# A two-layer decoder trunk on eight cores: weight casts issued in other places, the row work of the routing stage queued among the attention steps, and a last stage without a barrier before it

## What is computed

```python
for i in range(2):
    h = rms_norm(x, mix_norm_g[i])
    if i == 0:
        x = x + gmlp_mixer(h, ...)          # 1024 -> 6144 gelu, layer norm, 128x128 spatial mix, 3072 -> 1024
    else:
        k_band, v_band = shared_kv(x, kv_norm_g, w_kv, b_kv)     # previous and own block of 128
        x = x + swa_sink_attention(h, w_q, b_q, sinks, w_o, b_o, k_band, v_band)   # 16 heads of 64
    hn = rms_norm(x, ffn_norm_g[i])
    if i == 0:
        x = x + (silu(hn @ w_gate) * (hn @ w_up)) @ w_down       # 2816 wide
    else:
        x = x + moe_swiglu(hn, ...)          # top 2 of 8 experts, each 3584 wide
    x = x + (p[i] @ ple_w_proj[i]) * sigmoid(rms_norm(x, ple_norm_g[i]) @ ple_w_gate[i])
return rms_norm(x, final_norm_g)
```

## Time and profile before

| | us |
|---|---|
| median of three runs | 4339.06 |
| the runs | 4335.07, 4339.06, 4602.17 |
| the profiled execution, device time | 4306.77 |
| its span on the slowest core, 6 | 4305.2 |
| spans of the eight cores | 4209.3 to 4305.2 |

### The profile page before, as it was taken

One profiled execution on the slowest core, in us unless ns is written; L12 is line 12 of the kernel. 1 busy time (PEld: TensorE's weight loads), 2 busy tenths in 40 slices (PEclk: granted clock), 3 DMA queues, 4 the chain that ended last, 5 costly groups with the idle time before them and its releaser, 6 DMA issues.

```text
span 4305.2 us, 68531 instructions; the slowest of 8 cores (4209.3 to 4305.2 us)
## 1 busy us (share of the span) xinstructions
PE 3491.6 (81%) x20783; PEld 1990.8 (46%) x21030; DVE 1257.3 (29%) x2477; ACT 1030.7 (24%) x2319; POOL 588.5 (14%) x588
## 2 busy tenths in 40 slices
PE   4888848798899546755757999999999999999445
PEld 2555533354456323433653545546464646464222
DVE  2544531122222336745531111111111111111153
ACT  2555520011211322332421111111111111111133
POOL 1111122200000222221011000000010101010132
PEclk8999979899999777877858999999999999999767
DMA  9578769656655995999629897969696969795631
GB/s 158 89 117 129 108 134 229 179 84 97 100 86 91 195 177 80 112 109 109 106 110 259 201 241 172 255 163 265 170 264 173 254 185 255 196 239 141 203 124 59
DMA packets 368662, 691.02 MB, mean 161 GB/s; under 512 B 21642, under 2 KB 289708, under 8 KB 353836
## 3 DMA queue, kind: packets, MB, share of 16 engines
q0 software_dynamic: 280384, 299.40, 49.7%
q1 hardware_dynamic: 69772, 345.26, 24.0%
q10 hardware_dynamic: 18144, 41.95, 2.7%
HBM read 866.00 MB, written 212.21 MB: 250 GB/s over the span
## 4 chain that ended last, share of the span: by engine, by line
PE 71%; DMA 10%; issue 8%; DVE 5%; ACT 3%; POOL 2%; another core or an unknown queue 1%; DVEq 0%; SPq 0%; ACTq 0%; POOLq 0%
PE ps L247 68%; PE ps L250 3%; DMA arena<-xs 3%; DVE arena L270 2%; ACT arena L258 2%; DMA arena<-wgu 2%; DVE arena L261 1%; DMA arena<-gmlp_w_in 1%; ACT L258 1%; DMA xs<-arena 1%; DMA arena<-gmlp_w_out 1%; DMA arena<-ygs,arena 1%; POOL xgs L1354 1%; DMA arena<-gmlp_w_s 1%; POOL arena L291 1%
## 5 line engine op out<-in xcount | busy, mean ns | idle before, releaser
L247 PE MATMUL ps<-arena 128*128 128x512 bf16 (+7 forms) x18889 | 3321.9, 337 | 254.7 <-ACT arena L258 68.3
L247 PEld LDWEIGHTS ps<-arena 128*128 128x128 bf16 (+2 forms) x19136 | 1834.6, 103 | 1703.1 <-issue 454.8
L258 ACT ACTIVATE arena<-ps 128x512 f32<-128x512 f32 (+3 forms) x720 | 369.9, 516 | 1524.0 <-PE ps L247 1501.6
L261 DVE TENSOR_TENSOR arena<-arena,ps 128x512 bf16<-128x512 f32 (+3 forms) x619 | 351.3, 569 | 1239.3 <-PE ps L247 1140.1
L250 PE MATMUL ps<-arena 128*128 128x128 bf16 (+2 forms) x1894 | 210.7, 261 | 540.6 <-DVE arena L270 128.1
L250 PEld LDWEIGHTS ps<-arena 128*128 128x128 bf16 (+2 forms) x1894 | 165.2, 123 | 592.4 <-issue 583.1
L261 POOL TENSOR_TENSOR arena<-arena 128x512 f32<-128x512 f32 (+4 forms) x196 | 263.4, 1356 | 770.2 <-DVE arena L270 356.5
L258 ACT ACTIVATE arena<-arena 128x512 bf16<-128x512 bf16 (+9 forms) x300 | 193.6, 648 | 550.6 <-DMA arena<-xs 360.3
L1439 POOL DMA_DIRECT2D arena<-wdn x120 | 110.5, 925 | 1497.2 <-PE ps L247 1492.6
L275 ACT COPY arena<-ps 128x512 f32<-128x512 f32 (+1 forms) x166 | 134.1, 808 | 752.5 <-PE ps L247 588.3
L277 DVE COPY arena<-ps 128x512 f32<-128x512 f32 (+4 forms) x179 | 101.3, 569 | 696.6 <-PE ps L247 588.8
(11 more groups left out here) (38 smaller groups left out, 280.6 us busy)
## 6 DMA issues: line engine op xcount, KB each, us to landing
arena<-wgu SPq DMA_DIRECT2D x105, 2048.0 KB, 11.7
arena<-wdn POOLq DMA_DIRECT2D x120, 896.0 KB, 26.6
wgu<-moe_w_gate POOLq DMA_DIRECT2D x56, 1024.0 KB, 20.1
wgu<-moe_w_up POOLq DMA_DIRECT2D x56, 1024.0 KB, 24.4
...
arena<-xc SPq DMA_DIRECT2D x34, 512.0 KB, 11.1
xs<-arena ACTq DMA_DIRECT2D x34, 512.0 KB, 8.0
arena<-xs SPq DMA_DIRECT2D x34, 512.0 KB, 11.9
```

Of the source, the lines that this page charges most:

```text
L247: P.add("pe", lambda h: h.matmul(out, lhsT, rhs, start=start, stop=stop), reads=r, writes=w)
L258: P.add("act", lambda h: h.activation(out=out, in_=in_, func=func, scale=scale, **kw), reads=r, writes=w)
L261: P.add(eng, lambda h: h.tensor_tensor(out=out, in0=in0, in1=in1, op=op), reads=r, writes=w)
```

## The change

Five things are done at once.

1. **Casts.** G issues 34 instead of 27 (n % 3 == 2 instead of n % 4 == 3), F 43 instead of 27 (f % 3 == 2 instead of f % 6 == 5), E none instead of 12, so the attention stage has 35 left instead of 46.
2. **Zeros.** They are written in F's tiles 1 to 5 from SP's queue, 46 pieces of 256 KB, instead of 23 pieces of 512 KB in E.
3. **Rows and router.** The transposes back to rows, their copies, the stores to `xr_d`, the square sums and the router product leave the routing stage. They become three steps per block on the list `heavy` of the attention stage (`c_row` twice, `c_log`). Routing reloads the rows from `xr_d` (16 loads of 512 KB on SP's queue) and takes the roots for all blocks at once. `hrow` is computed after the token slots are known: four blocks before the expert numbers, twelve after. The scatters are recorded behind that. The attention stage has one buffer for the sine table instead of two.
4. **Routing to MoE.** Two pieces of gate and up weights are issued ahead of the barrier, into memory that routing does not use, and the barrier leaves them out.
5. **The last stage.** Its `epoch()` is gone. Its weights are loaded ahead of the last slot's `gate_up`, its 16 row buffers and eight inputs ahead of the last `down`, and the gathers wait for all stores to `yg_d`. The groups are replaced by one loop over 16 blocks in which normalisation runs one or two blocks ahead of the gate product and the combination six ahead; roots are still taken for four blocks at once.

```diff
-            if 0 < t < NG - 1 and n % 4 == 3:
+            if 0 < t < NG - 1 and n % 3 == 2:
                 PP.issue(1, [("vg", p, j, blk)])
...
-            if f % 6 == 5 and t > 0 and t + 1 < NFT:
+            if t > 0 and f % 2 == 0 and nz[0] < NROW:
+                DMA("sp", xg_d[nz[0]:nz[0] + 128, :], zt, "xst", ["zt"], [("xz", nz[0])])
+                nz[0] += 128
+            if f % 3 == 2 and t > 0 and t + 1 < NFT:
                 PP.issue(1, [("act", f - 1)])
...
         e_load(n + 7)
-        for _ in range(2):
-            if nz[0] < NROW:
-                n0 = nz[0]
-                nn = min(256, NROW - n0)
-                DMA("sp", xg_d[n0:n0 + nn, :].rearrange("(p a) d -> p (a d)", p=128), zt[:, 0:nn * D // 128], "xst", ["zt"], [("xz", n0)])
-                nz[0] += nn
-        if 2 <= n < 14:
-            PP.issue(1, [("tm", 1)])
...
+        def c_row(j, hf):
+            t0 = 128 + 128 * j
+            def f():
+                bk = nb()
+                q = rown[0] % 2
+                rown[0] += 1
+                for c in range(4):
+                    TR(bank(bk)[:, c * 128:(c + 1) * 128], xT[:, 4 * hf + c, t0:t0 + 128], ident32,
+                       xk([4 * hf + c], t0, 128) + ["ident32"], BK(bk))
+                CP("act" if q == 0 else "dve", xrh[q], bank(bk), BK(bk), [("xrh", q)])
+                DMA("sp", xr_d[j * 128:(j + 1) * 128, hf * 512:(hf + 1) * 512], xrh[q], "xw%d" % q, [("xrh", q)], [("xr_d", j, hf)])
+                ACT(junkr, xrh[q], AF.Square, [("xrh", q), "ssq2"], ["junkr", ("ssq2", j, hf)], accum=ssq2[:, 2 * j + hf:2 * j + hf + 1])
+            return f
+        def c_log(j):
...
+                for c in range(8):
+                    MM(bank(bk)[:, 0:NE], xT[:, c, t0:t0 + 128], wr[:, c, :], c == 0, c == 7, xk([c], t0, 128) + ["wr"], BK(bk))
+                CP("dve", L[:, j, :], bank(bk)[:, 0:NE], BK(bk), [("L", j)])
...
             if gb % 2 == 1:
                 heavy[1:1] = [c_wo(gb // 2, n_) for n_ in range(8)]
+                for j in (gb - 1, gb):
+                    heavy.extend([c_row(j, 0), c_row(j, 1), c_log(j)])
...
-    for j in range(16):
-        ... eight TR, CP act, CP dve, DMA to xr_d, ACT Square, eight MM, CP; roots and hrow per four blocks
+        DMA("sp", xrow[j], xr_d[j * 128:(j + 1) * 128, :], "tx%d" % j, [], [("xrow", j)])
+    RED(ssq, ssq2.rearrange("p (a b) -> p a b", b=2), ALU.add, [], ["ssq"])
+    TS("dve", rsd, ssq, 1.0 / D, ALU.mult, ["ssq"], ["rsd"], s2=EPS, op1=ALU.add)
+    ACT(rsd, rsd, AF.Sqrt, ["rsd"], ["rsd"])
...
     for _ in range(2):
         issue_gw()
+    barrier_keep([("gw", 0), ("gw", 1)], skip=("gw",))
+    issue_xg(0)
...
     for n in range(NS):
+        if n == NS - 1:
+            tail_weights()
         gate_up(n)
+        if n == NS - 1:
+            tail_rows()
         down(n)
-    epoch()
...
+    for k in range(NB):
+        t_norm2(k + 1)
+        t_norm1(k + 2)
+        t_gate(k)
+        for j in ([4, 5, 6] if k == 0 else [k + 6]):
+            if j < NB:
+                t_comb(j)
+        if k > 0:
+            t_sq(k - 1)
+        if k in (1, 5, 9, 13, 15):
+            js = list(range(13 if k == 15 else max(0, k - 4), k))
+            t_rs(([(sN, "sN", list(range(k + 3, k + 7)))] if k < 10 else []) + [(sF, "sF", js)])
+            ready += js
+        for _ in range(2 if len(ready) > 3 else 1):
+            if ready:
+                t_out(ready.pop(0))
```

247 lines of the change are left out of this document (130 added, 117 removed).

## The result

Two runs of the changed kernel took 4182.38 and 4183.72 us, two of the kernel before beside them 4335.07 and 4339.06; two more runs of each (4231.86 and 4250.97; 4602.17 and 4799.24) are of a slower state, in which cores of one die or both show a lower granted clock, and such runs are left out here and below. The ratio is 0.9645, 95% interval 0.9603 to 0.9686: about 154 us, 3.5%. The forecast was 4089, 250 us less than before, with a range of 4015 to 4190. The sign and the size of the two largest terms were right; about 100 us of the forecast did not come, and the time lies in the range only at its slow end. The profiled execution of the changed kernel took 4183.72 us, span 4181.9 on its slowest core, 5 (before: 4306.77).

The account below looks back on a forecast made before the run. No one engine bounds the whole: transfers bound E, waits the last stage. 3 + 8 - 56 - 70 - 6 + 55 - 85 + 3 - 102 = -250 took the median 4339 to 4089 us, range 4015 to 4190.

Parts of the forecast that it names:

- the two largest terms: Last stage, -102 us (174 instead of 276), and routing to MoE's first matmul, -85 us.
- Rival E: Routing: POOL excluded during `hrow`, scatters wait out each two-input product, 20 us instead of 4; whole 4105; chance 0.06.
- rival B: Last stage keeps the low clock: -55 us instead of -102, whole 4136; chance 0.13.
- +8 for five boundaries: F's tile boundaries: store, reload of `xf`, then `f_root` wait longer; +8 us, ends 0 and +50 (10 each).
- Rival F: F's boundary: store and reload each wait behind the casts, costing 405 us; whole 4486, slower; chance 0.02.
- 8 - 56 - 70 - 6: F's boundaries +8, E -56, attention's shorter stalls -70, attention's missing backlog -6 us.
- -70: stalls are 68 instead of 138: Attention: POOL's stalls before casts, two of 27 and 41 us instead of three totalling 138; -70 us.
- -6 for the backlog: Attention: backlog from the stage before gone, first loads land sooner; -6 us, router weights' scaling included.
- +55: Attention: row and router work moved in from routing costs 55 us, ends 15 and 85.
- Rival C: Attention gives the gain back: stalls stay at 138 us or rows cost all 85; together 4189; chance 0.13.
- the lower bound of 15: Attention's row and router work: low end of its cost, 15 us, a third of the full-clock price.
- Left as it is: MoE, 1754 us, not changed; forecast +3 us for the last stage's weights cast in the last slot, ends 0 and +15.

## Why the prediction was right and where it was wrong

**Routing, right.** -85 forecast, -87 and -88 measured, by its own steps: chain, 43 us of scatters, 11.5 to the first product. The price of DVE beside the scatters was +4 for 32 of them by a mean of 1.11 us; the scatters' mean was 1.03 (before, 0.97), so +2. Rival E, 20 us by exclusion, did not come. The rule of the Trainium skill on the shared interfaces (GPSIMD Engine Reference, Key points), that GpSimd contends with DVE instructions with two SBUF inputs, agrees with these means in direction only.

**The last stage, right in mechanism, 10 short.** The first sum came 5 us after the gathers began (9 forecast), the first gate product 15 after that (20). The step that failed is the block's pace: I took PE's 7.7, and steady blocks are 8.2 to 9.9 us apart, waiting for DVE; a root adds some 5 us more (3 forecast). From the first gate product to the end it was 164 us, where the forecast had 145. DVE's sums take 1.62 us where they took 1.44, with POOL's adds (1.70 against 1.59) denser beside them, and the normalisation waits behind a block's sums still. The clock of 0.78 was above 0.69 as said; rival B did not come.

**E, wrong by 38 on the mean.** The forecast was 131 for a stage without backlog; without one it is 140. The other 25 us are casts and the embedding's weights still landing when E began: on core 5 PE stood 17 us longer at E's start than with half the casts (33.18 against 16.31) and then waited 10 for the gate weight. In the changed kernel the weights needed 80.5 us from issue to landing (transfers issued from 1000 to 1400 us, core 5: kind, count, size, median us to landing):

```profile
wgu<-moe_w_up POOLq DMA_DIRECT2D x16, 1024.0 KB, 54.8
...
arena<-ple_w_gate POOLq DMA_DIRECT2D x1, 2048.0 KB, 80.5
```

I had priced F's transfers at 101 us per 100 us tile, saw that they just fit, and let the stage behind them start empty. Where a stage runs its engines at 1.0, what does not fit arrives in the next.

**F, wrong by 24.** The place was right, the wait of ACT at `f_root`, and the end of 10 us per boundary is just what came (9.5 to 11.3 in three of five). I took +8 for five boundaries, 1.6 each, because the wait had been 5.8 with casts already beside it; at a share of 0.55 that tells little of one at 0.94. Rival F, from 50 us per boundary on, was far off. F, E and attention together are the right unit: 1253 before, 1297 after; 45 more. In the kernel with the rows behind the loop and its stalls kept, F, E and the loop took 1252, so all the rest of the change brought 1 us there, where the forecast had 124 (8 - 56 - 70 - 6).

**Attention, wrong by 52, and for a reason that the sum hid.** The counting of stalls held in part: two more ahead of casts 86 and 100 were forecast; the one ahead of 100 came with 50 us on core 5 (41 forecast), the one ahead of 86 did not, and two came in F, where they cost nothing. So the stalls did fall, from 115 to 43 us on the mean, about the 70 that were forecast, and still the stage grew. The step that failed is "-70: stalls are 68 instead of 138", a stall taken at its full length. Shortening the stalls by 43 us in the kernel before gave 26 in attention and 4 at MoE's start; by 75 us beside the row work, with the casts at their old places, 23; and the 43 us left in the changed kernel cost it 14. The path, by runs: 513 before; 487 with the stalls shortened; 447 with 11 casts fewer, no backlog and 38 us of stalls on the mean; 530 with the row work and no stall; 544 with the changed kernel's 43 us of stalls. By this path the forecast's -70 is -12 (-26 + 14), its -6 for the backlog is -40 together with the 11 casts, and its +55 is +83, in sum +31. The 40 are not split further by any run.

The rows cost 52 or 83 us, as they stand beside a stall or not. I had +55 with an upper end of 85, and argued that nothing could hide in a stall, since nothing would stand queued that PE might do. The runs say the opposite for the changed kernel: beside its stall 31 us of the row work were free. For the kernel before this explains nothing, as it has no row work in attention; there the DMA share of 0.95 to 0.97 speaks for transfers as the bound, and no run took them away there. Rival C ("rows cost all 85") holds as a price, not as the sum that I gave it. That its 4189 is the forecast nearest to the 4183 measured is luck: its stalls of 138 us did not stay, and E, F and MoE, which it left alone, took 90 us more than forecast.

**The row work's price at the full clock** was set at half of that at the low one, 2.7 us per block as the lower bound of 15. No run showed the 8-column products at the full clock in a dense row; behind the loop the clock fell to 0.50 beside them, although PE was busy without a gap. That lower end rested on nothing.

**MoE, wrong by 28 on the mean.** "Left as it is" was true of its code. Its loss is a shortage of transfers, shown by the kernel with an eighth less to load, and it is the larger the nearer to each other two neighbouring cores start (the table above, a correlation). The kernel before showed the signs, and I did not look: its eight cores fall in two groups, 4209 to 4221 and 4299 to 4305 us, with MoE at 1707 and 1743. The slowest core's time speaks of the second group alone, and a change that brings the groups together lengthens MoE on all cores.

**The carrying to the median.** The profiled execution of before, 4306.8, was at the fast end; the runs of the same kernel beside the experiments go from 4309 to 4362. Of the changed kernel they agree within 2 us. So the pair of profiles shows 123 us of gain and the timed runs 154, and the differences of the ledger carry over to the median only within such a spread.
